# First mixer of a two-block kernel: unit order, start of the taps, place of the channel norm

## What is computed

```
h = rms_norm(x, norm1_g)
q, k, v, glu_a, glu_b = split(h @ w_in)            # 5 x 512 columns
q, k = rms_norm per head of 64
attn = stick_breaking_attention(q, k, v)           # 8 heads
c = glu_a * sigmoid(glu_b)
c = causal_depthwise_conv(c, conv_dw_w, conv_dw_b) # 31 taps
c = silu(layer_norm(c))
x = x + concat([attn, c]) @ w_out
```

## Time and profile before

| | us |
|---|---|
| median of 3 runs | 1227.64 (1227.39 to 1228.41) |
| the profiled execution | 1226.31 |
| its span on the core | 1224.6 |
| TensorE busy | 1188.5 |
| VectorE busy | 580.5 |
| ScalarE busy | 486.1 |
| GpSimd busy | 477.8 |

### The profile page before, as it was taken

How to read it: one execution, slowest core, us unless ns; L and a number is a source line. 1 busy time by engine, 2 the same in 40 slices (tenths; PEclk the granted TensorE clock), 3 DMA queues, 4 the chain that set the end, 5 groups by cost and what they waited for, 6 DMA issues and landing times.

```text
span 1224.6 us, 16511 instructions
## 1 busy us (share of the span) xinstructions
PE 1188.5 (97%) x6276; PEld 959.5 (78%) x6276; DVE 580.5 (47%) x886; ACT 486.1 (40%) x715; POOL 477.8 (39%) x251
## 2 busy tenths in 40 slices
PE   7998989999999999999999999999999999999997
PEld 6876757888888888888887777778888888888885
DVE  5698974165444444000375577943544445440003
ACT  6245474343333333112445745544433333332213
POOL 3541030744444444444583210007444344444443
PEclk9999999999999999999999999999999999999999
DMA  5421110323332222322232211213323333222211
GB/s 178 138 78 61 35 53 17 104 69 103 103 103 90 96 88 103 103 103 95 77 92 89 69 36 36 71 36 103 103 70 102 103 103 103 95 96 101 103 69 69
DMA packets 84603, 105.47 MB, mean 86 GB/s; under 512 B 2019, under 2 KB 77130, under 8 KB 84554
## 3 DMA queue, kind: packets, MB, share of 16 engines
q1 hardware_dynamic: 84394, 104.53, 25.9%
q10 hardware_dynamic: 160, 0.26, 0.1%
HBM read 102.43 MB, written 2.10 MB: 85 GB/s over the span
## 4 chain that ended last, share of the span: by engine, by line
PE 88%; DVE 5%; ACT 3%; issue 2%; DMA 1%; POOL 0%; SPq 0%; POOLq 0%; ACTq 0%; DVEq 0%
PE ps L1540 19%; PE ps L1542 18%; PE ps L1541 18%; PE ps L1868 10%; PE ps L1863 10%; PE ps L2052 3%; PE ps L1628 3%; DVE cy L1079 2%; PE ps L1674 2%; PE ps L2004 1%; PE ps L1695 1%; DMA w_raw<-in_w_in 1%; ACT w_hi L556 1%; PE ps L1919 1%; PE ps L1959 1%
## 5 line engine op out<-in xcount | busy, mean ns | idle before, releaser
L449 POOL TENSOR_TENSOR w_lo<-w_raw,w_hi 128x1024 fp32r<-128x1024 f32 x178 | 428.4, 2410 | 584.1 <-ACT w_hi L556 514.8
L1540 PE MATMUL ps<-h_hi,w_hi 128*128 128x512 f32 x936 | 371.0, 396 | 2.4 <-DVE w_lo L1005 1.6
L1541 PE MATMUL ps<-h_lo,w_hi 128*128 128x512 f32 x936 | 364.8, 390 | 0.0
L1542 PE MATMUL ps<-h_hi,w_lo 128*128 128x512 f32 x936 | 364.7, 390 | 0.0
L556 ACT ACTIVATE w_hi<-w_raw 128x1024 fp32r<-128x1024 f32 x190 | 200.0, 1055 | 326.3 <-PE ps L1542 145.4
L1540 PEld LDWEIGHTS ps<-h_hi,w_hi 128*128 128x128 f32 x936 | 175.8, 188 | 46.2 <-issue 6.8
L1542 PEld LDWEIGHTS ps<-h_hi,w_lo 128*128 128x128 f32 x936 | 175.8, 188 | 37.2
L1541 PEld LDWEIGHTS ps<-h_lo,w_hi 128*128 128x128 f32 x936 | 176.0, 188 | 35.5 <-issue 0.5
L1214 DVE TENSOR_TENSOR ps<-ps,rbs 128x512 f32<-128x512 f32 x88 | 61.5, 699 | 172.0 <-PE ps L1542 171.6
L738 ACT ACTIVATE cv<-ps,par 128x512 f32<-128x512 f32 x44 | 34.3, 780 | 183.9 <-DVE ps L1214 161.9
L1180 DVE TENSOR_TENSOR xT<-xT,ps 128x512 f32<-128x512 f32 x24 | 16.3, 685 | 154.9 <-PE ps L1868 106.7
(11 more groups left out here) (298 smaller groups left out, 1609.6 us busy)
## 6 DMA issues: line engine op xcount, KB each, us to landing
w_raw<-in_w_up SPq DMA_DIRECT2D x33, 1024.0 KB, 5.1
w_raw<-in_w_down SPq DMA_DIRECT2D x22, 1024.0 KB, 4.8
w_raw<-in_w_in SPq DMA_DIRECT2D x21, 1024.0 KB, 5.3
w_raw<-in_w_gate SPq DMA_DIRECT2D x11, 1024.0 KB, 5.1
w_raw<-in_w_out SPq DMA_DIRECT2D x8, 1024.0 KB, 5.2
xtok<-in_x SPq DMA_DIRECT2D x4, 512.0 KB, 5.1
out_dram<-obuf SPq DMA_DIRECT2D x8, 256.0 KB, 2.0
sq<-in_final_norm_w SPq DMA_DIRECT2D x1, 512.0 KB, 5.9
```

Source lines behind the costliest of these rows:

```text
L449: pool.tensor_tensor(unit_view(w_lo, at, down), unit_raw(at, down), unit_view(w_hi, at, down).bitcast(F32), ALU.subtract).then_inc(s_lo, 1)
L1540: pe.matmul(ps[:, bank, :], whi, hi, start=first, stop=False, skip_group_check=True)
L1541: pe.matmul(ps[:, bank, :], whi, lo, start=False, stop=False, skip_group_check=True)
L1542: mm = pe.matmul(ps[:, bank, :], wlo, hi, start=False, stop=last, skip_group_check=True)
```

## The change

Units 0 to 3 become gate 0, value 0, gate 1, value 1, each loaded by its own transfer of 128 columns, with a semaphore of its own (s_first) for units 0 and 2. ScalarE's takes follow. VectorE gates tile 0 as soon as both its units are taken, does 14 taps of it alone (SKEW), gates tile 1, does 17 taps of each in turn, then 14 of tile 1 alone. Tiles 2 and 3 begin after that, with 9 taps each ahead of scale_variance(0), where 2 each stood before, and all are done ahead of head 4. The channel norm (sums, mean, subtraction, squares, sums, variance) moves from behind head 5 and among heads 6 and 7 to beside heads 4 to 6, its first sums to bank 7. Units 15, tails(0) and tails(1), the values, and the first squares change places on TensorE and ScalarE. attended_hi of the first two pairs moves from ScalarE to VectorE. GpSimd's subtractions for units 20 to 23 wait for head 5 instead of for the last tap. The banks of `mix` change, spread(1) comes ahead of tails(7), and the steps of the channels for all four first output tiles come behind outputs(3). The number of matmuls stays.

```diff
-OUT_BANK = (0, 1, 2, 3, 6, 7, 2, 3)
+OUT_BANK = (6, 0, 1, 2, 3, 7, 1, 2)
+SKEW = 14
...
-            pair(0, cols(w_in, in_cols[0]), first=True)
+            def first_units(p, c0s):
+
+                for c, c0 in enumerate(c0s):
+                    sp.dma_start(unit_raw(2 * p + c, False),
+                                 w_in[0].rearrange("(k p) n -> p k n", p=P)[:, :, bass.ds(c0, P)]
+                                 ).then_inc(s_raw[p] if c else s_first[p], 16)
+
+            first_units(0, (B0, A0))
...
-            pair(1, cols(w_in, in_cols[1]), first=True)
+            first_units(1, (B0 + P, A0 + P))
...
-            pool.wait_ge(s_tap, 4 * CK)
+            pool.wait_ge(s_spl, 6)
             rests(U_OUT, 4)
...
@@ ScalarE @@
+            for u in range(8):
+                act.wait_ge(s_used, u + 1)
+                if u < 4:
+                    first, j = u % 2 == 0, u // 2
+                else:
+                    first, j = u < 6, 2 + u % 2
...
             square_qk(14, 15)
-            weights(0)
             take_qk(15, 7)
             square_qk(15, 16)
             lead(19)
+            weights(0)
             weights(1)
...
             front(4)
+            value(2)
             front(5)
-            value(2)
             value(3)
+            act.wait_ge(s_lp0, 1)
+            act.activation(nvar[:, 0, :], ps[:, 7, :], ACT.Copy).then_inc(s_lpd, 1)
             lead(20)
             lead(21)
             weights(4)
             lead(22)
+            channel_squares(range(2))
+            weights(5)
+            channel_squares(range(2, 4))
             lead(23)
-            weights(5)
-            attended_hi(0)
             front(6)
-            attended_hi(1)
+            act.wait_ge(s_lp, 1)
+            act.activation(nvar[:, 2, :], ps[:, 6, :], ACT.Copy).then_inc(s_lpc, 1)
             front(7)
...
@@ VectorE @@
+            def gate(j):
+                dve.wait_ge(s_take, 2 * j + 2 if j < 2 else 8)
+                dve.tensor_tensor(glu[:, j, PAD:PAD + SEQ], glu[:, j, PAD:PAD + SEQ], cy[:, j, :],
+                                  ALU.mult).then_inc(s_glu, 1)
+                dve.wait_ge(s_glu, j + 1)
...
             gate(0)
-            taps(0, 0, CK)
+            for n in range(SKEW):
+                tap(0, n)
             gate(1)
-            taps(1, 0, 2)
+            for n in range(SKEW, CK):
+                tap(0, n)
+                tap(1, n - SKEW)
+            for n in range(CK - SKEW, CK):
+                tap(1, n)
+            gate(2)
+            gate(3)
+            taps(0, 9)
             scale_variance(0)
-            taps(1, 2, 3)
+            taps(9, 10)
             scale_refine(0)
-            taps(1, 3, 4)
+            taps(10, 13)
             dve.wait_ge(s_cdve, 5)
             for n in range(4):
                 scale_qk(n)
-            taps(1, 4, 9)
+            taps(13, 18)
             head(0)
             head(1)
             dve.wait_ge(s_lo, 18)
             rest(U_IN + 18)
-            taps(1, 9, 12)
             rest(U_IN + 19)
             scale_variance(1)
-            taps(1, 12, 13)
+            taps(18, 20)
             scale_refine(1)
-            taps(1, 13, 15)
+            taps(20, 23)
             head(2)
             head(3)
-            taps(1, 15, 17)
             scale_qk(4)
             scale_qk(5)
-            taps(1, 17, 19)
+            taps(23, 25)
             scale_qk(6)
             scale_qk(7)
-            taps(1, 19, 28)
+            taps(25, CK)
             head(4)
             head(5)
-            taps(1, 28, CK)
-            attended_lo(0)
-            dve.wait_ge(s_lp0, 1)
-            dve.tensor_copy(nvar[:, 0, :], ps[:, 6, :]).then_inc(s_lpd, 1)
-            head(6)
             dve.wait_ge(s_mean, 1)
             for c in range(CT):
                 dve.tensor_tensor(cy[:, c, :], cy[:, c, :], ps[:, 6, :], ALU.subtract).then_inc(s_lc, 1)
-            attended_lo(1)
-            head(7)
-            attended_lo(2)
+            for p in range(2):
+                attended_hi(p)
+                attended_lo(p)
+            head(6)
             dve.wait_ge(s_stat, 1)
             variance(ps[:, 6, 0:TT], CT * P)
+            head_open(7)
             spread(1)
+            head_close(7)
+            attended_lo(2)
...
@@ TensorE @@
-            part(15, 7, range(4))
+            part(15, 7, range(8))
             tails(0)
-            part(15, 7, range(4, 8))
-            tails(1)
             pe.wait_ge(s_take, 15)
             statistics(1, 6)
+            tails(1)
+            value_rows(0, range(4))
             scores((2, 3))
-            value_rows(0)
+            value_rows(0, range(4, 8))
             value_rows(1)
...
             value_rows(3)
+            pe.wait_ge(s_tap, 4 * CK)
+            pe.wait_ge(s_vc, 3)
+            channel_sums(7, lnone[:], lambda c: cy[:, c, :], s_lp0)
             tails(4)
+            pe.wait_ge(s_lpd, 1)
+            pe.wait_ge(s_vc, 4)
+            pe.matmul(ps[:, 6, :], l32[:], nvar[:, 0, :], start=True, stop=True, skip_group_check=True).then_inc(s_mean, 1)
             tails(5)
...
+            tails(6)
+            spread(1, 6)
+            tails(7)
             pe.wait_ge(s_w, 7)
             pe.wait_ge(s_mlo, 3)
-            for m in range(3):
+            for m in range(1, 4):
                 mix(m, range(3), True, False)
-            spread(1, 6)
+            pe.wait_ge(s_ly, CT)
+            mix(0, range(3), True, False)
             outputs(3)
-            mix(3, range(3), True, False)
+            pe.wait_ge(s_clo, CT)
+            mix(0, range(4, KD), False, False)
             pe.wait_ge(s_mlo, 4)
-            for m in range(4):
-                mix(m, range(3, 4), False, False)
+            mix(0, (3,), False, True)
+            for m in range(1, 4):
+                mix(m, (4, 5, 6, 7, 3), False, True)
```

More of the change, by code:

```diff
@@ L168, in hybrid_blocks_kernel @@
         s_raw = [sem(f"s_raw{n}") for n in range(2)]
+        s_first = [sem(f"s_first{n}") for n in range(2)]
         s_hi = sem("s_hi")
@@ L340, in _, with pair @@
         def _(sp):
-            def pair(p, src, at=None, first=False):
+            def pair(p, src, at=None):
                 slot = p % 2 if at is None else at
-                if not first:
-                    sp.wait_ge(s_lo, 2 * p - 2)
+                sp.wait_ge(s_lo, 2 * p - 2)
                 sp.dma_start(w_raw[:, slot, :].rearrange("p (k n) -> p k n", n=src.shape[-1]),
@@ L589, in gain_hi @@
                                    scale=par[:, 0, gcol + k:gcol + k + 1]).then_inc(s_hhi, 1)
[L591 to L599, removed]
+            for u in range(8):
+                act.wait_ge(s_used, u + 1)
+                if u < 4:
+                    first, j = u % 2 == 0, u // 2
+                else:
+                    first, j = u < 6, 2 + u % 2
+                if first:
+                    act.activation(cy[:, j, :], ps[:, u % 4, :], ACT.Sigmoid).then_inc(s_take, 1)
+                else:
+                    act.activation(glu[:, j, PAD:PAD + SEQ], ps[:, u % 4, :], ACT.Copy).then_inc(s_take, 1)
+                lead(u + 4)
             def take_qk(u, bank):
@@ L673, in _, with channel_squares @@
             weights(3)
+            def channel_squares(cs):
+                for c in cs:
+                    act.wait_ge(s_lc, c + 1)
+                    act.activation(sqk(c), cy[:, c, :], ACT.Square).then_inc(s_lsq, 1)
             front(4)
+            value(2)
             front(5)
-            value(2)
             value(3)
+            act.wait_ge(s_lp0, 1)
+            act.activation(nvar[:, 0, :], ps[:, 7, :], ACT.Copy).then_inc(s_lpd, 1)
             lead(20)
@@ L681, in _ @@
             lead(22)
+            channel_squares(range(2))
+            weights(5)
+            channel_squares(range(2, 4))
             lead(23)
-            weights(5)
-            attended_hi(0)
             front(6)
-            attended_hi(1)
[L687 to L692, removed]
             act.wait_ge(s_lp, 1)
             act.activation(nvar[:, 2, :], ps[:, 6, :], ACT.Copy).then_inc(s_lpc, 1)
+            front(7)
+            attended_hi(2)
+            weights(6)
             weights(7)
@@ L1060, in gain_lo, with taps_done, tap @@
                                              hi.bitcast(F32), ALU.mult, ALU.subtract).then_inc(s_hlo, 1)
[L1062 to L1073, removed]
+            def gate(j):
[3 more added lines that the diff above has]
+                dve.wait_ge(s_glu, j + 1)
+            def taps_done(j, n):
+                if j == 0:
+                    return n if n <= SKEW else 2 * n - SKEW - 1
+                if j == 1:
+                    return SKEW + 2 * n if n <= CK - SKEW else CK + n
+                return 2 * CK + 2 * n - (3 - j)
+            def tap(j, n):
+                total = ps[:, 6 + j, :] if j < 2 else cy[:, j, :]
                 if n == 0:
@@ L1081, in tap, with taps @@
```

(37 more changed lines are left out.)

6 lines of the change are left out of this document (4 added, 2 removed).

## The result

The changed kernel takes 1233.66 us (median of 5, 1232.22 to 1235.58), the kernel before 1227.39 beside it (1226.19 to 1228.41): ratio 1.0048 with a 95% interval of 1.0035 to 1.0061. It is 6.3 us slower; 1233.0 was forecast. The profiled execution took 1235.58.

A forecast was written before the change was run, and what follows sets the result against it. TensorE was taken as the bound (97% of the span), its stops set by DVE. 7.7 behind at tails(0) - 10.6 old losses + 8.3 new losses = 5.4 us slower: 1231.7 profiled, 1233.0 timed median; range 1223.5 to 1239.5.

The forecast's parts named there:

- Start of DVE: First gate on VectorE: gate(0) is held by a GpSimd subtraction to 32.8 and ends at 33.5.
- Rival (d): Start: something else holds gate(0) to 41.4, so DVE starts no earlier; 5 to 8 us more, 1239; chance 0.02.
- A linked tap: Taps of one tile alone, each waiting for the one before: a tap of 0.74 takes 0.78 us.
- Rival (c): Tiles 0 and 1: a linked tap costs 0.66 like an unlinked one; 1231.5 us; chance 0.06.
- Up to the scores: DVE from gate(2) to scale_qk: subtractions delay taps, scale_variance(0) at 96.1, PE stops 4.5 and 5.4 us, scores at 111.8.
- rival (b): Taps around the scale: POOL does not hold DVE, scale_variance(0) starts at 89.5; 7.4 us faster, 1220.2; chance 0.20.
- rival (a): Ahead of the scores: subtractions 16 and 17 meet no tap, second stop 1.1 us; 1227.1, the same; chance 0.15.
- To the heads: Scores to tails(0): the 3.81 us stop goes, tails(0) ends at 127.8, PE 7.7 us behind.
- Behind it: After tails(0): the old kernel's losses of 10.6 us there are replaced by new losses of 8.3.
- The small stops: PE after tails(0): 0.4 for scale_qk(6), 0.5 for outputs(2), 0.7 for tails(6), 1.2 for tails(7).
- The stop behind outputs(3): PE waits at once for s_clo, queued behind attended_hi(3) and attended_lo(3): 3.8 us, plus 1.7 of clock.
- (e): Whole kernel, the main forecast: subtractions hold DVE's taps and PE stops; 5.4 us slower, 1233.0 timed; chance 0.57.

The follow-up runs named there:

- the start alone: Kernel before with only the new unit order, single transfers, early taps of tile 0 and skew, the rest in old order: 1227.45 us, ratio 1.0001.
- The kernel without 16 and 17: Changed kernel with GpSimd subtracting only 8 columns of the weights of units 16 and 17: 1227.49 us, ratio 0.9999.
- the one without all four: Changed kernel with GpSimd subtracting only 8 columns of the weights of units 14 to 17: 1221.86 us, ratio 0.995.
- mixing ahead of the last tails: Changed kernel with DVE taps reordered, channel parts first, norm behind scores(6, 7), outputs(2) and three mix steps ahead of tails(7): 1228.01 us, ratio 1.0002.
- scale earlier: Changed kernel with only DVE's order redone, three taps per tile ahead of scale_variance(0) instead of nine, six ahead of scale_qk instead of thirteen: 1230.57 us, ratio 1.0025.
- the three kernels without subtractions: Changed kernel with 8-column subtractions for units 14 and 15, 16 and 17, or all four: 1228.6, 1227.49 and 1221.86 us.
- scale earlier and the end: Changed kernel with fewer DVE taps ahead of scale_variance(0) and scale_qk, and channel parts ahead of attended_hi(3) and attended_lo(3): 1220.74 us, ratio 0.9943.

## Why the prediction was right, step by step

**Start of DVE.** gate(0) was forecast to end at 33.5 and ended at 30.75 + 2.74 = 33.5. Rival (d) is out, and the start alone makes no difference.

**A linked tap.** Forecast 0.78: 13 take 10.26 us, 0.79 each. Thirty in alternation take 19.84, 0.66 each, though every one of these waits on a semaphore as well. So waiting for the instruction directly in front costs 0.13 us, and waiting for the one before that nothing. Rival (c) is out. The Trainium skill (VectorE: DVE Perf Modes, The DRAIN you can't avoid) measured copies with a semaphore after each at no extra cost; that doesn't carry over to these linked operations, 0.79 against 0.66.

**Up to the scores.** gate(2) 78.7, measured 78.86; scale_variance(0) 96.1 (91.6 + 4.4 is 96.0), measured 96.04; six taps 8.3, measured 8.39; stops 4.5 and 5.4, measured 4.52 and 5.28. Each subtraction was priced at 2.2 (2.1 for units 16 and 17), and the kernels without them show 2.1 to 2.2. That settles rival (b), and rival (a) with it: subtractions 16 and 17 did meet the taps. The kernel without 16 and 17 takes 1227.49, as (a) had it (1227.1), the one without all four 1221.86 where (b) had 1220.2; (b) also took gate(0) as free, which in that kernel is still held and takes 2.74 us. The Trainium skill (SBUF — State Buffer, Who interferes with whom) has an exclusive lock between VectorE and GpSimd. The trace agrees, with taps of up to 2.95 us instead of 0.74. It adds that with both queues full the turns alternate for whole subtractions: four of them beside taps come 11.14 / 4 = 2.8 us apart (mixing ahead of the last tails), one tap and one subtraction. The taps with their total in PSUM are free of it here too, as their line of the listing shows (durations in ns: shortest, middle, longest, then the starts):

```profile
L1101 DVE SCALAR_TENSOR_TENSOR cy<-glu,par,cy x60: 737/742/2945, 83.3 to 162.0; 128x512 f32<-128x512 f32 x60
L1101 DVE SCALAR_TENSOR_TENSOR ps<-glu,par,ps x58: 742/747/756, 34.4 to 77.4; 128x512 f32<-128x512 f32 x58
```

**To the heads.** tails(0) was to end at 127.8 and ended at 127.3: 7.2 behind, where the sum had 7.7.

**Behind it.** The small stops were forecast at 0.4, 0.5, 0.7 and 1.2 and came at 0.93, 0.62, 0.34 and 0.69: 2.8 against 2.6 in all, right by cancellation, since each was worked from several durations. The stop behind outputs(3) was 3.83 for a forecast of 3.8. The term of the sum that this trace shows otherwise is the clock behind it: 3.0 us, not 1.7, which I had copied from one other stop of the same length. Behind the same stop the profiled executions of scale earlier and of the three kernels without subtractions lost 1.6 to 1.7, so 1.7 was the usual value and this execution had another. With it the new losses are 2.6 + 3.8 + 3.0 = 9.4 instead of 8.3, and 7.2 - 10.6 + 9.4 = 6.0, beside the 5.85 that the residual row shows.

**The whole.** The mechanism of (e) was right. The bounds of the sum, taken as independent, give about 1229 to 1237, a little narrower than the recorded 1228.5 to 1238; 1233.66 lies in both. The profiled execution is 3.3 us longer again, from the clock at a place the change doesn't touch (below); in the medians of five the difference is 6.3. The profiled one is also the slowest of the five, so how near its 5.85 comes to the forecast 5.4 is in part luck: with 1.7 us of clock behind the stop, all else alike, the rows would give about 4.6 (an estimate from these numbers).

**Why slower, then.** The early start frees 5 us of DVE. The change spends it on taps ahead of the scale, and more of it than there is: 18 taps instead of 4, two subtractions among them, then six instead of two with two more. The second reason is separate: the stop behind outputs(3).

## What to carry to other kernels

An engine that starts earlier gains only what its order does with it: here the same start was worth nothing in the old order, and with six tap pairs ahead of the scores instead of thirteen, and the end mended, it belongs to a kernel of 1220.7 us. Count what the other user of SBUF has queued beside every stretch of VectorE work on the path, reckon with nearly its whole length for each such operation (2.1 to 2.2 us for one of 2.4), and place waits so that the two do not meet: one wait was worth 10.5 us. When work that used to fill a wait is moved ahead, look at what then stands directly behind the wait, and in which order the other queues serve it.

## What was not expected of the hardware

**Clock behind a stop.** A stop of 3.81 us was followed by 1.7 us of clock loss before, one of 3.83 by 3.0 after, in the third window above. Five kernels have this same stop of 3.82 or 3.83 us behind outputs(3). Over the 12 us from its end the granted clock was 0.86 in three of them and 0.87 in one, a loss of 1.6 to 1.7 us, and 0.75 in the change, 3.0 us. What decides it isn't known; price such a stop at 1.7 us of clock and allow for 3.0.

**Clock with TensorE busy.** In the changed kernel's profiled execution, far behind the change, between the first block and the second:

```profile
614.20 1.05 PE L1734 MATMUL ps<-ones,htmp 128*128 128x1 f32 x8
615.12 2.23 PE L1734 MATMUL ps<-ones,sq 128*128 128x1 f32 x16
```
```profile
618.00:620.00 2.00, 2.00 (x6) 1.52 (x6) 1.33 (x3) 0.00 (x0) 1.20 (x2) 0.50 0.00 0
600.00:630.00 30.00, 29.99 (x129) 24.25 (x128) 20.81 (x27) 15.55 (x24) 20.75 (x22) 0.89 0.24 71
```

TensorE isn't idle for a moment, yet at the end of 24 matmuls of a single column the clock falls to 0.50, the lower of the two levels (1.2 instead of 2.4 GHz), and 30 x 0.11 = 3.3 us are lost. The kernel before does the same matmuls at 608 and stays at full clock:

```profile
600.00:630.00 30.00, 29.99 (x143) 24.60 (x142) 26.10 (x35) 16.16 (x26) 23.42 (x30) 1.00 0.22 71
```

Over the twelve profiled executions this window has 1.00 four times, 0.94 four times and 0.89 four times: 0, 1.8 or 3.3 us, whatever the edit was. A profiled pair can thus differ by 3.3 us at a place that no edit touches. That the single columns cause the fall isn't shown: in all eight executions that have it, it comes within 1.5 us of their end, and in the other four the same columns go by without it. Whether a kernel's own timing decides which case it gets, and whether that explains the 4 to 5 us of clock in scale earlier and the end, stays open: timed executions have no such rows, and no run varied it alone.
